# A transformer block pair on one core: first projections of two mixes on the input without the norm's factor

## The chip, the cores and the metric

One core of a Trainium2 chip runs the whole program. The metric is the device time of one execution in microseconds, here called us; lower is better. Beside the time of a whole execution there is one profiled execution, from which all rows come; their times are us from the start of its span.

## What is computed

Two transformer blocks, one behind the other, on 512 positions of 1024 features, in fp32. What matters here are the two places where a norm is followed by a projection. Cut to that:

```python
def rmsnorm(x, w):                       # rms_norm of the second block is the same
    return x * lax.rsqrt(jnp.mean(x * x, axis=-1, keepdims=True) + EPS) * w

def first_block(x, ...):
    u = rmsnorm(h, norm_mix_pre[i])
    (qa, ka, va, za, ...) = jnp.split(u @ w_in[i], offs, axis=-1)
    ya = gdn_mixer(qa, ka, va, ...)      # qkv: causal_dwconv of width 4, then silu
    ...
def second_block(x, ...):
    x = x + 0.5 * swiglu(rms_norm(x, ffn1_norm[l]), ...)
    z = rms_norm(x, mix_norm[l]) @ w_in[l] + b_in[l]
    a_q, a_k, a_v, ... = jnp.split(z, SPLIT_POINTS, axis=-1)
    ...
```

The factor `rsqrt(mean(x*x))` is one number per position; the gain `w` is one per feature. The projection sums over features, so the factor can stand ahead of the projection or behind it.

## The kernel before

**Layout.** Features lie on the 128 partitions, positions along a row: `h`, `u_hi` and `u_lo` are 8 chunks of 128 x 512. Every fp32 product is three products in a rounded format: a value is split in a high half (rounded) and a low half (the rest), and `hi*hi + hi*lo + lo*hi` is summed in a PSUM bank. `u_hi` and `u_lo` are the halves of the normed input, `w_hi` and `w_lo` those of the weights.

**Weights.** They come as a stream of slabs of 512 KB, eight 128 x 128 tiles each. SyncE (SP) loads slab s into one of four `raw` buffers (L591), when the slab four before it has been split; ScalarE rounds it to `w_hi` (L1254, `feed_to`), GpSimd (POOL) subtracts for `w_lo` (L625), TensorE may use it then. There are five split buffers. ScalarE rounds slabs at places in its queue that the code names; `feed(name, m)` rounds up to some slabs ahead of a group.

**Groups.** A group is one output chunk: 8 input chunks x 3 products of 128 x 512, 5.4 us. `dense` runs the groups of a layer one after another (L701 to L703). For layers in `ABREAST` (qkv, w_o, up, up1, wq, up2) the first four groups run abreast in four banks: for each input chunk i the products of all four (L686 to L688), so that a chunk of the input is needed only every 2.7 us. `dense(..., row=name)` puts the norm's sums ahead of step 6 and the spreading of its factor ahead of step 7 of this phase. Banks: group g uses bank g % 4 by default; TensorE waits for the reader of the bank's last group (`freed`). Banks 4 to 7 are `misc` 0 to 3. down1 ends in bank 2, `out` in bank 1.

**A norm.** ScalarE squares the chunks (L1317), VectorE adds them up (`add_squares`, L1792, which runs behind by two chunks with three buffers), TensorE sums over partitions (`row_sums`, L734), ScalarE takes the root (L1321), VectorE the reciprocal (L1769, L1820), TensorE spreads it over partitions into a bank (`row_spread`, L741). `stay_busy` (L748) is filler for TensorE.

**Two ways to use it.** At pre0 (first projection qkv) and pre3 (wq) the kernel waits for the factor: VectorE makes the product of h, gain and factor (`norm_apply`, L1779), ScalarE rounds it to `u_hi` (L1285, `split_hi`), VectorE subtracts for `u_lo` (L1783), chunk by chunk. At pre1, pre2 and pre4 (up, up1, up2) it doesn't wait: ScalarE writes `u_hi` as h times gain (L1296, `late_act`), VectorE `u_lo` (L1796, `late_lo`), the abreast phase runs, and the factor, copied to `r_sb` (L1822, `late_inverse`), multiplies the outputs (L1829). The outputs of these layers are all multiplied; nothing else reads u there.

**Behind qkv.** For each of 12 groups ScalarE copies the bank times a tap (L1355), VectorE adds three shifted taps (L1867), ScalarE does silu (L1359). For the first 8, q and k, ScalarE squares (L1367), TensorE sums over partitions (`length_sum`, L1181, called behind group m for chunk m - 2, behind group 4 for chunks 0 to 2), ScalarE copies that to `lens` (L1371). TensorE goes on with the next group only behind its sums. Then come rows1 and the delta rule (`gdn`), which reads u too (nq, nk and more projections).

**Behind wq.** VectorE adds the bias (L2173); wk goes to ScalarE (L1610), then `wv` (L720, VectorE L2177) and the attention with a window of 128.

## Time and profile before

| | us |
|---|---|
| median of 3 runs | 2319.16 (2318.23 to 2320.23) |
| profiled execution, whole time | 2319.29 |
| its span, first to last instruction | 2317.5 |
| TensorE (PE) busy | 2238.6 (97%) |
| VectorE (DVE) / ScalarE (ACT) / GpSimd (POOL) busy | 887.0 / 892.8 / 905.1 |
| mean granted TensorE clock | 0.991 of 2.4 GHz |

A timeline row is: start, duration, engine, line of the kernel, operation, output<-inputs, shapes, count; in brackets the idle time of the engine ahead of it and what ended it. PEld is TensorE's weight load, ACTq and SPq are the queues' issues of DMAs. A granted clock of 1.00 is 2.4 GHz, 0.50 is 1.2 GHz. Matmuls overlap: one of 128 x 512 is shown with 0.39 us and starts 0.227 us behind the one before it.

### The profile page before, as it was taken

The page shows a single profiled execution, that of the slowest core. Times are in us where ns is not written, and L with a number is a line of the kernel's source. Part 1 is how long each engine was busy: PE and PEld are TensorE (multiplying, and loading weights), DVE is VectorE, ACT ScalarE, POOL GpSimd, SP SyncE. Part 2 cuts the span into 40 slices and gives each one's busy share as a digit, 9 for nine tenths or more (in the row PEclk, how much of TensorE's full clock was granted, in tenths as well). Part 3 has the DMA queues.
Part 4 walks back from the last instruction along what each step waited for, and adds up shares of the span by engine and source line. Part 5 has one row for each costly group of instructions (what it writes and reads, how often), then busy time and mean ns, then how long its engine had stood idle before and what let it go on. Part 6 is the DMA issues. An engine that isn't in the chain of part 4 may idle for free.

```text
span 2317.5 us, 27646 instructions
## 1 busy us (share of the span) xinstructions
PE 2238.6 (97%) x11180; PEld 1834.1 (79%) x11180; DVE 887.0 (38%) x1561; ACT 892.8 (39%) x1479; POOL 905.1 (39%) x387
## 2 busy tenths in 40 slices
PE   7999789999999999999999999999999999999998
PEld 6789677778788888777888888767888888888887
DVE  5374444544655540225333103262645223323201
ACT  4544544554444442243322222364336433232221
POOL 3321232224454454445444443214442444444442
PEclk9999989999999999999999999999999999999999
DMA  4200231114132333222233332113331232323331
GB/s 156 82 28 28 94 118 47 55 50 134 63 108 92 99 112 92 69 91 82 91 95 105 100 99 88 55 37 101 92 100 37 82 93 90 109 91 98 99 103 46
DMA packets 54990, 197.94 MB, mean 85 GB/s; under 512 B 6352, under 2 KB 7248, under 8 KB 54480
## 3 DMA queue, kind: packets, MB, share of 16 engines
q1 hardware_dynamic: 52416, 188.77, 26.1%
q10 hardware_dynamic: 2448, 7.41, 0.9%
q8 instruction: 89, 1.46, 0.3%
q14 instruction: 37, 0.30, 0.0%
HBM read 194.06 MB, written 2.10 MB: 85 GB/s over the span
## 4 chain that ended last, share of the span: by engine, by line
PE 90%; DVE 5%; ACT 2%; issue 1%; POOL 1%; DMA 1%; ACTq 0%; SPq 0%; DVEq 0%
PE dense L701 16%; PE dense L703 16%; PE dense L702 16%; PE misc L701 5%; PE misc L702 5%; PE misc L703 5%; PE misc L662 3%; PE misc L664 2%; PE misc L663 2%; PE dense L686 1%; PE dense L687 1%; PE dense L688 1%; DVE slot L1792 1%; PE dense L827 1%; PE dense L976 1%
## 5 line engine op out<-in xcount | busy, mean ns | idle before, releaser
L625 POOL TENSOR_TENSOR w_lo<-raw,w_hi 128x1024 fp32r<-128x1024 f32 x349 | 853.8, 2459 | 1260.3 <-ACT w_hi L1254 1204.8
L1254 ACT ACTIVATE w_hi<-raw 128x1024 fp32r<-128x1024 f32 x352 | 361.8, 1050 | 159.9 <-PE dense L703 100.1
L701 PE MATMUL dense<-u_hi,w_hi 128*128 128x512 f32 x928 | 366.8, 395 | 8.6 <-DVE ug_lo L2158 7.5
L703 PE MATMUL dense<-u_hi,w_lo 128*128 128x512 f32 x928 | 361.8, 390 | 0.0
L702 PE MATMUL dense<-u_lo,w_hi 128*128 128x512 f32 x864 | 336.3, 389 | 0.0
L701 PEld LDWEIGHTS dense<-u_hi,w_hi 128*128 128x128 f32 x928 | 174.6, 188 | 50.6 <-DVE ug_lo L2158 7.9
L701 PE MATMUL dense<-a_hi,w_hi 128*128 128x512 f32 x528 | 205.4, 389 | 0.0
L702 PE MATMUL dense<-a_lo,w_hi 128*128 128x512 f32 x528 | 205.4, 389 | 0.0
L703 PE MATMUL dense<-a_hi,w_lo 128*128 128x512 f32 x528 | 205.4, 389 | 0.0
L703 PEld LDWEIGHTS dense<-u_hi,w_lo 128*128 128x128 f32 x928 | 174.6, 188 | 36.7
L702 PEld LDWEIGHTS dense<-u_lo,w_hi 128*128 128x128 f32 x864 | 162.2, 188 | 35.5 <-issue 2.4
L701 PE MATMUL misc<-u_hi,w_hi 128*128 128x512 f32 x400 | 155.8, 390 | 0.0
L702 PE MATMUL misc<-u_lo,w_hi 128*128 128x512 f32 x400 | 155.6, 389 | 0.0
L703 PE MATMUL misc<-u_hi,w_lo 128*128 128x512 f32 x400 | 155.6, 389 | 0.0
L702 PEld LDWEIGHTS dense<-a_lo,w_hi 128*128 128x128 f32 x528 | 99.1, 188 | 20.7
L703 PEld LDWEIGHTS dense<-a_hi,w_lo 128*128 128x128 f32 x528 | 99.1, 188 | 20.7
L701 PEld LDWEIGHTS dense<-a_hi,w_hi 128*128 128x128 f32 x528 | 99.1, 188 | 20.2
L1792 DVE TENSOR_TENSOR slot<-slot,slot 128x512 f32<-128x512 f32 x63 | 54.2, 860 | 142.2 <-ACT slot L1317 139.0
L1844 DVE SCALAR_TENSOR_TENSOR h<-dense,h 128x512 f32<-128x512 f32 x24 | 16.6, 692 | 240.1 <-PE dense L703 240.1
L1332 ACT ACTIVATE slot<-dense 128x512 f32<-128x512 f32 x30 | 18.0, 599 | 211.9 <-DVE dense L1829 211.9
L703 PEld LDWEIGHTS misc<-u_hi,w_lo 128*128 128x128 f32 x400 | 75.1, 188 | 15.7
L701 PEld LDWEIGHTS misc<-u_hi,w_hi 128*128 128x128 f32 x400 | 75.1, 188 | 15.6
(419 smaller groups left out, 3924.8 us busy)
## 6 DMA issues: line engine op xcount, KB each, us to landing
raw<-in_weights SPq DMA_DIRECT2D x352, 512.0 KB, 3.5
h<-in_x SPq DMA_DIRECT2D x4, 512.0 KB, 6.3
alibi<-in_alibi ACTq DMA_DIRECT2D x1, 2048.0 KB, 7.4
h<-in_x ACTq DMA_DIRECT2D x2, 1024.0 KB, 6.3
out<-result SPq DMA_DIRECT2D x8, 256.0 KB, 2.2
masks_in<-in_masks ACTq DMA_DIRECT2D x1, 512.0 KB, 9.2
p_raw<-in_p ACTq DMA_DIRECT2D x1, 512.0 KB, 3.5
mvb<-in_mvb ACTq DMA_DIRECT2D x1, 512.0 KB, 3.1
```

The lines of the kernel that those rows point to most:

```text
L625: nc.gpsimd.tensor_tensor(w_lo[:, s % SPLITS, :, :], raw[:, s % RAWS, :, :], w_hi[:, s % SPLITS, :, :].bitcast(F32), ALU.subtract).then_in ...
L662: mm(out, hi, src_hi[:, i, :], start=(i == 0), stop=False)
L663: mm(out, hi, src_lo[:, i, :], start=False, stop=False)
L664: last = mm(out, lo, src_hi[:, i, :], start=False, stop=(i == k - 1))
L686: mm(out, hi, src_hi[:, i, :], start=(i == 0), stop=False)
L687: mm(out, hi, src_lo[:, i, :], start=False, stop=False)
L688: last = mm(out, lo, src_hi[:, i, :], start=False, stop=(i == k - 1))
L701: mm(out, hi, src_hi[:, i, :], start=(i == 0), stop=False)
L702: mm(out, hi, src_lo[:, i, :], start=False, stop=False)
L703: last = mm(out, lo, src_hi[:, i, :], start=False, stop=(i == k - 1))
L1254: f(w_hi[:, s % SPLITS, :, :], raw[:, s % RAWS, :, :], ACT.Copy).then_inc(w_part, 1)
L1792: TT(slot[2][:, :], (slot[2] if c > 1 else sq[0])[:, :], sq[c % 3][:, :], ALU.add).then_inc(ms_acc, 1)
```

## The change

At qkv and at wq the abreast phase now runs on h times gain, without the factor, as at up, up1 and up2. The factor multiplies the four outputs in their banks: `first_scaled` at qkv, ahead of ScalarE's tap copy, with the new semaphore `qs_done`; at wq ahead of the bias. Unlike there, other groups and layers read u behind this phase. So `u_hi` and `u_lo` are written a second time, now with the factor (`rewrite` on VectorE, `rewrite_hi` on ScalarE), each chunk as soon as TensorE has read it in the abreast phase (`u_read`), and group 4 waits chunk by chunk for the second writing (`again`). The sums stand ahead of step 4 and the spread ahead of step 5 at qkv, 2 and 3 at wq. pre0's factor is copied to a place of its own, `r_first`.

With it: slab 0 is loaded ahead of x and slab 1 in the middle of it; masks and rowmask are issued behind the root of pre0; ScalarE waits for vec, ident and ones before its first work; the filler ahead of qkv is 6 products in place of 30, that ahead of wq is gone; qkv uses five banks, wq six, wk and wv banks of their own. All numbers of `u_ready` behind are shifted. The diff, without the shifted numbers:

```diff
+        for c in range(12):
+            bank_of[START["qkv"][1] + c] = (0, 1, 2, 3, 7)[c % 5]
+        for c in range(8):
+            bank_of[START["wq"][1] + c] = c % 6
+        for c in range(2):
+            bank_of[START["wk"][1] + c] = 2 + c
+        for c in range(NT):
+            bank_of[START["wv"][1] + c] = (4, 5, 0, 1)[c]
...
         def _(sp):
-            for i in range(4):
-                sp.dma_start(h[:, 2 * i:2 * i + 2, :], t["x"][:, 2 * i:2 * i + 2, :]).then_inc(x_loaded[i], 16)
-            for s in range(NSLABS):
-                if s >= RAWS:
-                    sp.wait_ge(*split_of(s - RAWS))
+            for s, pairs in ((0, (0, 1)), (1, (2, 3)), (2, ()), (3, ())):
+                sp.dma_start(raw[:, s, :, :], t["weights"][s]).then_inc(w_loaded[s], 16)
+                for i in pairs:
+                    sp.dma_start(h[:, 2 * i:2 * i + 2, :], t["x"][:, 2 * i:2 * i + 2, :]).then_inc(x_loaded[i], 16)
+            for s in range(RAWS, NSLABS):
+                sp.wait_ge(*split_of(s - RAWS))
...
-                            mm(out, hi, src_hi[:, i, :], start=(i == 0), stop=False)
+                            first = mm(out, hi, src_hi[:, i, :], start=(i == 0), stop=False)
+                            if again is not None and m == 0 and i >= 1:
+                                first.then_inc(u_read, 1)
...
+                        if again is not None and m == ahead:
+                            pe.wait_ge(u_ready, again + i + 1)
...
-            norm_row("pre0", busy=(16, 2, 12))
+            stay_busy(6)
...
-            dense("qkv", u_hi, u_lo, (u_ready, 0), length_sum)
+            dense("qkv", u_hi, u_lo, (u_ready, 0), length_sum, row="pre0", row_at=(4, 5), again=DC)
...
-            norm_row("pre3", busy=(8, 2, 8))
-            dense("wq", u_hi, u_lo, (u_ready, 4 * DC))
+            dense("wq", u_hi, u_lo, (u_ready, 5 * DC), row="pre3", row_at=(2, 3), again=6 * DC)
...
+            def early_act():
+                f(spare_col, one_col, ACT.Sqrt)
+                feed_to(1)
+                for c in range(DC):
+                    act.wait_ge(x_loaded[c // 2], 16)
+                    f(u_hi[:, c, :], h[:, c, :], ACT.Copy, scale=V("mix_pre", c)).then_inc(u_part, 1)
+                    square("pre0", c, h)
+                    if c in (1, 5, 7):
+                        feed_to(rounded[0] + 1)
+                root("pre0", misc[3])
+
+            def rewrite_hi(k0, name):
+                slabs = (START[name][0] + 4 * DC - 1) // SLAB + 1
+                for c in range(DC):
+                    feed_to(slabs + 1 + c // 2)
+                    act.wait_ge(ux_done, k0 + c + 1)
+                    if c < DC - 1:
+                        act.wait_ge(u_read, (DC - 1) * k0 // DC + c + 1)
+                    else:
+                        act.wait_ge(dense_done, group_of(name, 3))
                     f(u_hi[:, c, :], slot[4 + c % 2][:, :], ACT.Copy).then_inc(u_part, 1)
...
+            act.wait_ge(pool_step, 3)
+            act.wait_ge(in_loaded, 48)
+            early_act()
             act.dma_start(masks_in[:, :, :], t["masks"]).then_inc(c_loaded, 16)
             act.dma_start(rowmask[:, :], t["rowmask"]).then_inc(c_loaded, 16)
-            act.wait_ge(pool_step, 3)
-            norm_act(0, 0)
-            split_hi(0, "qkv")
+            rewrite_hi(0, "qkv")
...
+                    if c < 4:
+                        act.wait_ge(qs_done, c + 1)
                     f(slot[c % 2][:, :], out_bank("qkv", c)[:, :], ACT.Copy,
...
-            norm_act(3, 24, "down1")
-            split_hi(8, "wq")
+            late_act(3, 24, "mix2", "wq", "down1")
+            rewrite_hi(8, "wq")
...
-            def norm_apply(n, gain, k0):
-                inverse(f"pre{n}")
+            def rewrite(gain, k0, factor):
                 for c in range(DC + 1):
                     if c < DC:
                         if c >= 2:
-                            dve.wait_ge(u_ready, k0[1] + c - 1)
-                        STT(slot[4 + c % 2][:, :], h[:, c, :], V(gain, c), misc[2][:, :], ALU.mult, ALU.mult)\
+                            dve.wait_ge(u_ready, k0 + c - 1)
+                        STT(slot[4 + c % 2][:, :], h[:, c, :], V(gain, c), factor[:, :], ALU.mult, ALU.mult)\
                             .then_inc(ux_done, 1)
...
-            for i in range(4):
-                dve.wait_ge(x_loaded[i], 16)
-            for c in range(1, DC):
-                add_squares("pre0", c)
-            norm_apply(0, "mix_pre", (0, 0))
+            for c in range(DC):
+                late_lo(c, "mix_pre", 0)
+                if c >= 2:
+                    add_squares("pre0", c - 1)
+            add_squares("pre0", DC - 1)
+            late_inverse("pre0", r_first)
+            rewrite("mix_pre", DC, r_first)
+
+            def first_scaled(c):
+                dve.wait_ge(dense_done, group_of("qkv", c))
+                out = out_bank("qkv", c)
+                TT(out[:, :], out[:, :], r_first[:, :], ALU.mult).then_inc(qs_done, 1)
 
+            first_scaled(0)
             for c in range(12):
+                if c + 1 < 4:
+                    first_scaled(c + 1)
                 dve.wait_ge(cv_lin, c + 1)
...
-            add_half("down1", 0.5, "pre3")
-            norm_apply(3, "mix2", (0, 32))
+            add_half("down1", 0.5, "pre3", ("mix2", 5 * DC))
+            late_inverse("pre3")
+            rewrite("mix2", 6 * DC, r_sb)
             for c in range(8):
                 dve.wait_ge(dense_done, group_of("wq", c))
+                if c < 4:
+                    out = out_bank("wq", c)
+                    dve_link(dve, TT(out[:, :], out[:, :], r_sb[:, :], ALU.mult))
```

## Rows read from the trace of the kernel before

**Rows 1.** The page: share of each engine in the chain that ended last.
```profile
PE 90%; DVE 5%; ACT 2%; issue 1%; POOL 1%; DMA 1%; ACTq 0%; SPq 0%; DVEq 0%
```
**Rows 2.** The start: timeline, then one stretch of busy time by engine.
```profile
8.85 5.21 PE L748 MATMUL misc<-ident,ones 128*128 128x128 f32 x32 [8.85 <-DMA ones<-in_ones]
...
10.00:12.00 2.00, 2.00 (x12) 2.00 (x11) 0.74 (x2) 0.05 (x1) 0.00 (x0) 1.00 1.02 400
```
**Rows 3.** The chain behind the abreast phase of qkv; the table load; the sums.
```profile
44.48 0.70 ACT slot L1355
...
45.86 1.28 ACT L1359 ACT_TABLE_LOAD   x1
...
53.14 1.88 PE L1181 MATMUL misc<-slot,ones 128*128 128x512 f32 x4
54.26 0.63 ACT L1367 ACTIVATE slot<-qkv 128x512 f32<-128x512 f32 x1 [1.63 <-PE misc L1181]
...
56.05 0.79 PE L701 MATMUL dense<-u_hi,w_hi 128*128 128x512 f32 x1
```
**Rows 4.** VectorE by line: duration in ns, min/median/max.
```profile
L1796 DVE SCALAR_TENSOR_TENSOR u_lo<-h,vec,u_hi x24: 735/750/2866, 597.1 to 1944.6; 128x512 fp32r<-128x512 f32 x24
...
L1779 DVE SCALAR_TENSOR_TENSOR slot<-h,vec,misc x16: 740/748/751, 20.2 to 1425.0; 128x512 f32<-128x512 f32 x16
...
L1829 DVE TENSOR_TENSOR dense<-dense,r_sb x30: 693/700/700, 1071.3 to 2179.4; 128x512 f32<-128x512 f32 x30
...
L1867 DVE SCALAR_TENSOR_TENSOR slot<-dense,vec,slot x36: 737/749/752, 45.2 to 101.6; 128x511 f32<-128x511 f32 x12, 128x510 f32<-128x510 f32 x12, 128x509 f32<-128x509 f32 x12
```
**Rows 5.** Timelines: GpSimd and VectorE side by side, the steps of ScalarE, pre3's first product.
```profile
19.05 7.49 POOL L625 TENSOR_TENSOR w_lo<-raw,w_hi 128x1024 fp32r<-128x1024 f32 x3 [0.23 <-ACT w_hi L1254]
21.62 2.66 DVE L1783 TENSOR_TENSOR u_lo<-slot,u_hi 128x512 fp32r<-128x512 f32 x1
...
1057.75 2.87 DVE L1796 SCALAR_TENSOR_TENSOR u_lo<-h,vec,u_hi 128x512 fp32r<-128x512 f32 x1
...
1943.89 0.72 ACT L1296 ACTIVATE u_hi<-h,vec 128x512 fp32r<-128x512 f32 x1 [3.25 <-DVE h L1844]
...
1945.04 1.04 ACT L1254 ACTIVATE w_hi<-raw 128x1024 fp32r<-128x1024 f32 x1
...
1415.55 1.41 DVE L1779 SCALAR_TENSOR_TENSOR slot<-h,vec,misc 128x512 f32<-128x512 f32 x2 [1.25 <-PE misc L741]
...
1425.64 1.48 DVE L1783 TENSOR_TENSOR u_lo<-slot,u_hi 128x512 fp32r<-128x512 f32 x2
```
**Rows 6.** Stretches: length; PE, PEld, DVE, ACT, POOL busy (x); granted clock; DMA share; GB/s.
```profile
24.34:46.31 21.97, 21.97 (x96) 17.86 (x96) 11.27 (x15) 8.46 (x12) 9.29 (x4) 1.00 0.40 121
289.24:295.06 5.82, 5.82 (x27) 5.82 (x28) 5.73 (x8) 1.77 (x2) 2.39 (x1) 0.50 0.62 187
1063.06:1069.89 6.83, 6.83 (x21) 5.67 (x21) 0.18 (x1) 4.38 (x5) 4.62 (x2) 0.50 0.17 53
1410.39:1418.08 7.69, 6.50 (x54) 5.93 (x52) 4.62 (x8) 3.10 (x5) 2.36 (x1) 1.00 0.01 3
1418.08:1439.97 21.89, 21.89 (x97) 18.13 (x98) 10.61 (x16) 7.93 (x10) 9.51 (x4) 1.00 0.39 113
1472.60:1473.75 1.15, 0.17 (x2) 0.03 (x1) 0.00 (x0) 0.94 (x2) 0.00 (x0) 1.00 0.81 224
1942.96:1967.01 24.05, 23.94 (x114) 19.73 (x113) 5.30 (x9) 7.18 (x9) 8.09 (x5) 1.00 0.21 64
619.33:622.74 3.41, 3.41 (x11) 2.83 (x11) 0.18 (x1) 2.80 (x4) 1.52 (x1) 0.50 0.00 0
```
**Rows 7.** Waits between wk and wv: engine line waited for: us, times, longest.
```profile
PE dense L720 <- ACT wk L1610: 1.0, 1, 1.0
```
**Rows 8.** Timeline: sums, and the copy of the factor, at pre1.
```profile
618.64 1.26 PE L734 MATMUL misc<-ones,slot 128*128 128x1 f32 x8 [3.34 <-DVE slot L1792]
...
625.08 0.69 DVE L1822 COPY r_sb<-misc 128x512 f32<-128x512 f32 x1 [4.67 <-PE misc L741]
```

More of the change, by code:

```diff
@@ L242, in build @@
         r_sb = arena("r_sb", 86, [S])
+        r_first = arena("r_first", 24, [S])
         p_raw = at("p_raw", 88 * KB, [2, S])
@@ L314, in build @@
         u_ready = sem("u_ready")
+        u_read = sem("u_read")
+        qs_done = sem("qs_done")
         po_copy = sem("po_copy")
@@ L667, in dense_part, with dense @@
                     last.then_inc(dense_done, 1)
-            def dense(name, src_hi, src_lo, k_ready=None, after=None, row=None):
+            def dense(name, src_hi, src_lo, k_ready=None, after=None, row=None, row_at=(DC - 2, DC - 1), again=None):
                 tile, g0 = START[name]
@@ L675, in dense @@
                     for i in range(k):
-                        if row and i == k - 2:
+                        if row and i == row_at[0]:
                             row_sums(row, misc[3])
-                        if row and i == k - 1:
+                        if row and i == row_at[1]:
                             row_spread(row, misc[3])
@@ L1199, in _ @@
             norm_row("post0", busy=(6, 2, 14))
-            dense("up", u_hi, u_lo, (u_ready, DC), row="pre1")
+            dense("up", u_hi, u_lo, (u_ready, 2 * DC), row="pre1")
             dense("down", a_hi, a_lo, (a_ready, 0))
@@ L1208, in _ @@
             for m in range(DC):
-                dense(f"ple_gate{m}", u_hi, ug_lo, (u_ready, 2 * DC) if m == 0 else None)
+                dense(f"ple_gate{m}", u_hi, ug_lo, (u_ready, 3 * DC) if m == 0 else None)
                 if 1 <= m < DC - PLE_AHEAD + 1:
@@ L1213, in _ @@
             norm_row("post2", busy=(10, 2, 14))
-            dense("up1", u_hi, u_lo, (u_ready, 3 * DC), row="pre2")
+            dense("up1", u_hi, u_lo, (u_ready, 4 * DC), row="pre2")
             dense("down1", a_hi, a_lo, (a_ready, FC))
-            norm_row("pre3", busy=(8, 2, 8))
-            dense("wq", u_hi, u_lo, (u_ready, 4 * DC))
+            dense("wq", u_hi, u_lo, (u_ready, 5 * DC), row="pre3", row_at=(2, 3), again=6 * DC)
             dense("wk", u_hi, u_lo)
@@ L1236, in _ @@
             dense("out", mg_hi, mg_lo, (mg_ready, 0))
-            dense("up2", u_hi, u_lo, (u_ready, 5 * DC), row="pre4")
+            dense("up2", u_hi, u_lo, (u_ready, 7 * DC), row="pre4")
             dense("down2", a_hi, a_lo, (a_ready, 2 * FC))
@@ L1270, in norm_act @@
                         feed(layer, c)
-                    if n == 0:
-                        act.wait_ge(x_loaded[c // 2], 16)
-                    else:
-                        act.wait_ge(h_ready, ready + c + 1)
-                    square(f"pre{n}", c, h)
-                if n == 0:
-                    feed_to(1)
-                root(f"pre{n}")
-            def split_hi(k0, name):
-                feed_to((START[name][0] + 4 * DC - 1) // SLAB + 1)
-                for c in range(DC):
-                    act.wait_ge(ux_done, k0 + c + 1)
+                    act.wait_ge(h_ready, ready + c + 1)
+                    square(f"pre{n}", c, h)
+                root(f"pre{n}")
+            def early_act():
[15 more added lines that the diff above has]
+                        act.wait_ge(u_read, (DC - 1) * k0 // DC + c + 1)
+                    else:
+                        act.wait_ge(dense_done, group_of(name, 3))
                     f(u_hi[:, c, :], slot[4 + c % 2][:, :], ACT.Copy).then_inc(u_part, 1)
@@ L1363, in _ @@
                     if i == 0:
-                        act.wait_ge(u_ready, 8)
+                        act.wait_ge(u_ready, 2 * DC)
                     if i >= 2:
@@ L1814, in post_apply, with late_inverse @@
                         add_squares(pre, c - 2)
-            def late_inverse(name):
+            def late_inverse(name, factor=r_sb):
                 r = NORMS.index(name)
@@ L1821, in late_inverse @@
                 dve.wait_ge(ms_row, r + 1)
-                dve_link(dve, v.tensor_copy(r_sb[:, :], misc[3][:, :]))
+                dve_link(dve, v.tensor_copy(factor[:, :], misc[3][:, :]))
             def ffn_gate(n, name):
@@ L1871, in _ @@
             dve.wait_ge(c_loaded, 32)
-            dve.wait_ge(u_ready, 8)
+            dve.wait_ge(u_ready, 2 * DC)
             dve_link(dve, v.tensor_copy(masks[:, :, :], masks_in[:, :, :]))
@@ L2165, in _ @@
             add_squares("post2", DC - 1)
-            post_apply(2, "ple_post", mo_a, "pre2", "ffn1", 3 * DC)
+            post_apply(2, "ple_post", mo_a, "pre2", "ffn1", 4 * DC)
             late_inverse("pre2")
             ffn_gate(1, "up1")
-            add_half("down1", 0.5, "pre3")
-            norm_apply(3, "mix2", (0, 32))
+            add_half("down1", 0.5, "pre3", ("mix2", 5 * DC))
+            late_inverse("pre3")
+            rewrite("mix2", 6 * DC, r_sb)
             for c in range(8):
                 dve.wait_ge(dense_done, group_of("wq", c))
+                if c < 4:
+                    out = out_bank("wq", c)
+                    dve_link(dve, TT(out[:, :], out[:, :], r_sb[:, :], ALU.mult))
                 TS(wq[:, c, :], out_bank("wq", c)[:, :], V("b_wq", c), ND ** -0.5, ALU.add, ALU.mult).then_inc(wq_done, 1)
@@ L2356, in _ @@
                 TT(mg_lo[:, m, :], ma[:, m, :], mg_hi[:, m, :].bitcast(F32), ALU.subtract).then_inc(mg_ready, 1)
-            add_half("out", 0.5, "pre4", ("ffn2", 5 * DC))
+            add_half("out", 0.5, "pre4", ("ffn2", 7 * DC))
             late_inverse("pre4")
```

7 lines of the change are left out of this document (3 added, 4 removed).

## The prediction

> **What bounds the kernel.** The page first: TensorE is 90% of the chain that ended last [rows 1]. So a change pays only where TensorE stands still, or where something in front of a standing TensorE becomes shorter or longer. I then read the chain and the timeline at the two places that the change touches.
>
> At the start, TensorE waits for the `ones` load until 8.85 us [rows 2], does filler and the sums of pre0, and begins its first projection at 24.34. It does the four abreast groups in 21.97 us [rows 6], then group 4 (the fifth), and then, from 53.14, the three length sums. These wait for what VectorE and ScalarE make of groups 0 to 2: the chain of work that ended last runs through the tap copy L1355 at 44.48 [rows 3]. Group 5 begins at 56.05. From there to rows1 TensorE hardly stands, so the start of group 5 is my milestone for stage one. Its inputs: group 0 ready at 44.48, group 5 at 56.05, 11.57 us later.
>
> Before wq TensorE has its last `down1` product issued at 1410.39 and its first wq product at 1418.08: 7.69 us, filler included, then 21.89 us for the abreast phase, and 1.15 us between wk and wv [rows 6], most of it a wait for `wk` [rows 7]. The clock was granted in full in all of these stretches.
>
> **Stage two: what goes.** It becomes what the kernel already does from `out` to up2: there the abreast phase with sums and spread inside it took 24.05 us from the last product of `out` [rows 6], with no idle time ahead. Of that some 0.3 us was a wait for bank 1, which `out` had just used and up2 wants with its fourth product (an estimate: a sum of 0.7 on VectorE less the 0.45 of TensorE's products in between); down1 ends in bank 2, wanted with the seventh, so I take 23.7. Against 7.69 + 21.89 = 29.58 that is 5.9 us less. The rewrite begins behind the spread at product step 3 and must be ahead of group 4. By the steps below it takes 18 us from `r_sb` and that is ready about 11 us into the phase: the last halves come at 29.0, while group 4 wants them at 23.7 + 7 x 0.68 = 28.5. I take 0.5 us off the gain: 5.4. The four extra products on VectorE (0.70 us each, L1829 [rows 4]) and the wq bias behind them are done at about 35.5; group 6, the first that wants their bank, comes at 35.1 but needs only the first of the four. The new banks free wv of the wait for `wk`: 1.0 us. **Stage two: -6.4 us** (bounds -7.9, if the sums inside the phase cost nothing more than their 1.05 us and nothing waits, and -4.5, if the rewrite is 2 us later).
>
> **Stage one, the start.** SyncE now sends slab 0 first. The loads move about 400 GB/s [rows 2], 1.3 us for 512 KB, so the last pair of x, 2.1 MB into SyncE's queue before, comes at most two slabs, 2.6 us, later; it is there by 14 (an estimate), and ScalarE wants it only at about 18: nothing. ScalarE's work waits for `ones`, 8.85; a table load was done in the idle time ahead of another wait (45.86 [rows 3]), so I count it as done; if not, 1.28 us more. Then 0.2 + 1.0 (`w_hi`), pairs of `u_hi` and square of 1.15 us (1943.89 to 1945.04), and `w_hi` of 1.04 after the second, sixth and eighth pair [rows 5].
>
> GpSimd splits slab 0 from 10.15 to 12.5. And here is what I hold for decisive: **VectorE instructions with both inputs in SBUF and GpSimd's split keep each other out.** `u_lo` L1783, 0.74 us for one of two at the end of pre3, took 2.66 at 21.62, beside the splits from 19.05 to 26.54; L1796, 0.75 in the median, took 2.87 at 1057.75. As three splits in a row took 7.49, with one VectorE instruction let in between two of them, I take it that they take turns, a split being 2.4. Instructions with an input in PSUM, L1779, L1829, L1867, never took longer than 0.752 [rows 4, 5]. Laid out in this way: first `u_lo` at 13.1 (held by split 0), second 13.8, third 16.7 (held by split 1), first add 17.3, for which square 3 waits 2.3 us. ScalarE's last square ends at 8.85 + 0.2 + 3 x 1.0 + 8 x 1.15 + 2.3 = 23.6. VectorE's sixth add ends about 25.0, split 3 holds the port to 27.3, then `u_lo`, add, add: **29.1**. TensorE starts at 13.2, 11.1 us earlier, is through four of the eight steps at 13.2 + 4 x 2.73 = 24.1, and stands before the sums until 29.1. Bounds: 24.1 (no turn lost) and 30.4.
>
> **Sums to factor.** From sums to the end of the copy of the factor took 7.13 us at 618.64 (to 625.77), behind an idle time of 3.34 us [rows 8] and with the clock at half, 1.2 GHz, for 3.41 us of work [rows 6]. At full clock that would be 1.7 less, 5.4; with the half clock of 6.83 us that pre2 shows [rows 6] 8.8. Here TensorE has stood 5.0. I take 7.1: **36.2**.
>
> **The rewrite.** Eight times product (0.75), `u_hi` copy and `u_lo` (0.74): 11.6 us in all from 1415.55 to 1427.12 [rows 5], 1.4 a chunk. But the product read the factor from PSUM; now it reads `r_first`, so all of VectorE's rewrite has both inputs in SBUF. ScalarE rounds a slab ahead of chunks 2, 4 and 6, so GpSimd splits three slabs (2.4 us each) in the middle of it, each keeping VectorE out for nearly all of its time: 7.2, less the 1.0 in which VectorE would have waited for ScalarE anyway: 6.2, total 18.0. (The slab ahead of chunk 0, and the 1.4 us of issuing masks and rowmask, now in ScalarE's queue behind the root, lie before the factor.) Bounds 11.6 and 19. **54.2**.
>
> **From rewrite to group 5.** VectorE takes its queue in order: the first scaling, and with it every convolution, stands behind the last `u_lo`. Then the old chain of 11.57 us with 0.70 for the first scaling, 1.4 for two more between the convolutions, less the 1.63 us in which square 2 had waited for TensorE [rows 3], which it now doesn't, and 0.3 for the silus behind: 12.3. Meanwhile TensorE ends its abreast groups near 44 and group 4 with the last halves at about 55, then stands for 11 us but for single sums. **Group 5: 66.5**, 10.5 later than 56.05. At 289.24 TensorE came back from a long idle time to a half clock for 5.82 us of work [rows 6], which costs half of that, 2.9 (bounds 0 and 3.4). **Stage one: +13.4.** rows1 now waits for group 10's convolution, a copy of 0.70 and three of 0.75 behind its group [rows 3, 4], within the 5.4 us that group 11 takes: nothing.
>
> **Sum.** The profiled execution took 2319.29 us, 0.13 over the median of 2319.16, with a span of 2317.5. 2319.3 + 13.4 - 6.4 = **2326.3**.
>
> **Rules of the Trainium skill.** L1796 takes 0.750 us with `h` and `u_hi` in SBUF, L1779 0.748 with one source in PSUM [rows 4]. The Trainium skill, Vector Engine (DVE) Microarchitecture Reference, section Points that are easy to get wrong, says that this form with two SBUF sources that aren't bf16 runs at half the rate. By that the product of the rewrite would slow down; the trace speaks against it.
>
> **Rivals.**
> - The forecast, locks and turns as laid out, 2324 to 2332: 0.55.
> - Part of the turns fall between VectorE's instructions: sums at 27, factor 5.45 behind, rewrite 15, group 5 at 59.8, clock 1.7: +5.4 - 6.4, 2318.3, and what lies within 4.6 us of before. For it: half of the instructions at L1796 took 0.75 or less [rows 4], in stretches in which GpSimd worked too. 0.25.
> - The other side: the new order of GpSimd and VectorE meets hardly at all. Sums 24.1, factor 29.6, rewrite over at 41.2, group 5 at 53.5, clock 1.7: -0.8 - 6.4, **2312.1**. It decides through the end of the rewrite: with 12.3 and 2.9 behind it and 6.4 gained in stage two, the change wins if that end is before 56.05 + 6.4 - 15.2 = 47.3. 0.12.
> - The rewrite's cover holds also for the scalings (VectorE gets them done without holding up TensorE), so that the abreast phase alone decides: 13.2 + 23.7 = 36.9 against 46.31, -9.4 - 6.4: 2303.5. The order of VectorE's queue speaks against it. 0.04.
> - The product with both sources in SBUF takes double, 8 x 0.75 = 6.0 more in the rewrite: 2332.3. Against it stands L1796 [rows 4]. 0.04. (It is what the rule of the Trainium skill above would do.)
>
> **Range and chances.** 4.6 us is 0.2% and about what a measurement can tell. Faster by more: 0.12 + 0.04 less rounding, 0.15; within: 0.25; slower by more: 0.55 + 0.04, 0.60. The range goes from the fast rival, 2311, to 2332 and leaves out 2303.5, the doubled product and the tail of my bounds.
>
> **What would show it.** In the new profile: first L686 near 13.2; sums of pre0 near 29 with 5 us of idle TensorE ahead and a half clock around it; the copy of `r_first` near 36; some of the rewrite's products or `u_lo` at 2 to 3 us instead of 0.75; first scaling near 54; TensorE idle between group 4 and group 5, whose first product is near 66. Near wq: no idle behind down1, wv right behind wk. I am wrong if all instructions of the rewrite take 0.75 us, or if group 5 starts before 60.

## The result and the profile after

The changed kernel takes **2322.93 us** (median of 20 runs, 2319.66 to 2325.80), the kernel before 2318.93 (20 runs beside them, 2316.82 to 2320.37). Ratio 1.0017, 95% interval 1.0011 to 1.0023: 4.0 us or 0.17% slower. The profiled execution of after has a span of 2321.4 us where before had 2317.5, at a mean granted clock of 0.987.

Only two places of the program changed their length by more than the clock makes. I follow one and the same weight slab through both traces, by the start of its rounding on ScalarE (`w_hi`, L1254 before, L1268 after), and subtract:

```
slab   before     after      after - before
18     130.15     142.17     +12.0   behind stage one (qkv, rows1)
42     375.75     388.90     +13.2
210   1396.90    1408.54     +11.6   ahead of stage two
228   1527.92    1531.88      +4.0   behind stage two (wq, wk, wv)
359   2277.34    2281.31      +4.0   last slab
```

Stage one costs 12.0 us, stage two gives 7.7 by this measure, and what lies between wanders by 1.5.

**The start.** Timelines of after: ScalarE, VectorE, GpSimd and TensorE; start, duration, engine, line, operation, in brackets the idle time ahead and what ended it.

```profile
8.81 1.28 ACT L1291 ACT_TABLE_LOAD   x1 [8.81 <-DMA ones<-in_ones]
...
18.32 0.63 ACT L1343 ACTIVATE slot<-h 128x512 f32<-128x512 f32 x1 [2.11 <-DVE slot L1820]
...
11.90 3.00 DVE L1824 SCALAR_TENSOR_TENSOR u_lo<-h,vec,u_hi 128x512 fp32r<-128x512 f32 x2 [2.90 <-ACT u_hi L1295]
15.11 2.58 DVE L1824 SCALAR_TENSOR_TENSOR u_lo<-h,vec,u_hi 128x512 fp32r<-128x512 f32 x1 [0.21 <-ACT u_hi L1295]
...
18.21 0.74 DVE L1824 SCALAR_TENSOR_TENSOR u_lo<-h,vec,u_hi 128x512 fp32r<-128x512 f32 x1
...
22.82 2.38 DVE L1824 SCALAR_TENSOR_TENSOR u_lo<-h,vec,u_hi 128x512 fp32r<-128x512 f32 x1 [0.60 <-ACT u_hi L1295]
...
25.73 2.87 DVE L1824 SCALAR_TENSOR_TENSOR u_lo<-h,vec,u_hi 128x512 fp32r<-128x512 f32 x1
...
11.33 2.35 POOL L636 TENSOR_TENSOR w_lo<-raw,w_hi 128x1024 fp32r<-128x1024 f32 x1 [10.89 <-ACT w_hi L1268]
14.54 2.60 POOL L636 TENSOR_TENSOR w_lo<-raw,w_hi 128x1024 fp32r<-128x1024 f32 x1 [0.85 <-ACT w_hi L1268]
...
22.25 2.40 POOL L636 TENSOR_TENSOR w_lo<-raw,w_hi 128x1024 fp32r<-128x1024 f32 x1 [5.12 <-ACT w_hi L1268]
25.48 2.57 POOL L636 TENSOR_TENSOR w_lo<-raw,w_hi 128x1024 fp32r<-128x1024 f32 x1 [0.82 <-ACT w_hi L1268]
...
14.30 0.79 PE L697 MATMUL dense<-u_hi,w_hi 128*128 128x512 f32 x1 [2.58 <-DVE u_lo L1824]
14.89 0.63 PE L700 MATMUL dense<-u_lo,w_hi 128*128 128x512 f32 x1
...
30.05 1.05 PE L749 MATMUL misc<-ones,slot 128*128 128x1 f32 x8 [2.73 <-DVE slot L1820]
```

Four of the eight `u_lo` take long: 2.34 at 11.90 (the first of the two in that row), 2.58 at 15.11, 2.38 at 22.82 and 2.87 at 25.73. Each starts within 0.6 us behind the start of a split; where GpSimd is idle, at 18.21, one takes 0.74. TensorE starts 10 us earlier than at 24.34 [rows 6] and then stands 2.73 us ahead of the sums. The sums themselves come at 30.05.

**The rewrite and what follows.** The same engines, where before the chain of [rows 3] ran:

```profile
36.48 0.69 DVE L1850 COPY r_first<-misc 128x512 f32<-128x512 f32 x1 [4.86 <-PE misc L756]
37.21 1.41 DVE L1807 SCALAR_TENSOR_TENSOR slot<-h,vec,r_first 128x512 f32<-128x512 f32 x2
...
40.77 2.77 DVE L1807 SCALAR_TENSOR_TENSOR slot<-h,vec,r_first 128x512 f32<-128x512 f32 x1
43.46 0.68 DVE L1811 TENSOR_TENSOR u_lo<-slot,u_hi 128x512 fp32r<-128x512 f32 x1
...
50.35 2.73 DVE L1807 SCALAR_TENSOR_TENSOR slot<-h,vec,r_first 128x512 f32<-128x512 f32 x1
53.01 1.46 DVE L1811 TENSOR_TENSOR u_lo<-slot,u_hi 128x512 fp32r<-128x512 f32 x2
54.39 1.29 DVE L1896 TENSOR_TENSOR dense<-dense,r_first 128x512 f32<-128x512 f32 x2
...
40.31 2.68 POOL L636 TENSOR_TENSOR w_lo<-raw,w_hi 128x1024 fp32r<-128x1024 f32 x1 [4.80 <-ACT w_hi L1268]
45.23 2.54 POOL L636 TENSOR_TENSOR w_lo<-raw,w_hi 128x1024 fp32r<-128x1024 f32 x1 [2.24 <-ACT w_hi L1268]
50.01 2.52 POOL L636 TENSOR_TENSOR w_lo<-raw,w_hi 128x1024 fp32r<-128x1024 f32 x1 [2.24 <-ACT w_hi L1268]
...
59.59 2.07 PE L1196 MATMUL misc<-slot,ones 128*128 128x512 f32 x2 [4.10 <-ACT slot L1396]
62.41 2.07 PE L1196 MATMUL misc<-slot,ones 128*128 128x512 f32 x2 [0.75 <-ACT slot L1396]
65.80 2.05 PE L1196 MATMUL misc<-slot,ones 128*128 128x512 f32 x2 [1.32 <-ACT lens L1400]
66.86 1.42 PE L716 MATMUL dense<-u_hi,w_hi 128*128 128x512 f32 x1
```

The rewrite goes from 37.21 to 54.47, 17.3 us. Three of its eight products take 2.7 to 2.8 us, each beside one of the three splits; the other products take 0.75 and all `u_lo` 0.68 or 0.69. Behind it stand the first scaling at 54.39 and then, one after another, the three length sums L1196, each for a square L1396 or a `lens` copy. Group 5 starts at 66.86, where before it started at 56.05 [rows 3].

**Stage two.** TensorE, VectorE and GpSimd of after, then the abreast phase as a stretch (length; busy time of PE, PEld, DVE, ACT, POOL; clock, DMA share, GB/s):

```profile
1426.86 0.95 PE L749 MATMUL misc<-ones,slot 128*128 128x1 f32 x8
1430.54 1.05 PE L756 MATMUL misc<-ident,small 128*128 128x128 f32 x8
1445.06 0.39 PE L716 MATMUL misc<-u_hi,w_hi 128*128 128x512 f32 x1
...
1431.62 0.69 DVE L1850 COPY r_sb<-misc 128x512 f32<-128x512 f32 x1 [3.30 <-PE misc L756]
1435.92 2.77 DVE L1807 SCALAR_TENSOR_TENSOR slot<-h,vec,r_sb 128x512 f32<-128x512 f32 x1
1448.20 1.47 DVE L1811 TENSOR_TENSOR u_lo<-slot,u_hi 128x512 fp32r<-128x512 f32 x2
...
1435.46 2.68 POOL L636 TENSOR_TENSOR w_lo<-raw,w_hi 128x1024 fp32r<-128x1024 f32 x1 [3.95 <-ACT w_hi L1268]
...
1421.42:1445.06 23.64, 23.64 (x113) 19.81 (x112) 16.10 (x19) 9.85 (x15) 10.48 (x4) 1.00 0.28 77
```

No PE row carries a bracket: TensorE runs from down1 into wq and on into group 4 without standing. It takes 23.64 us where before took 7.69 + 21.89 [rows 6], 5.94 less. The rewrite has the same three slow products and is over 17.3 us behind its start (1432.35 to 1449.67), and here nobody waits for it: group 4 wants the last chunk at 1445.06 + 7 x 0.68 = 1449.8, 0.15 us later.

### The profile page after: what moved, and what is told of

Its sections match the earlier page's. It is cut to its first block, busy times and chain, and to the rows that moved or that the text cites. A ratio compares the mean times of both kernels' runs of the same rounds, so it can differ in the third digit from the quotient of the medians.

```text
span 2321.4 us, 27525 instructions
## 1 busy us (share of the span) xinstructions
PE 2236.2 (96%) x11096; PEld 1826.8 (79%) x11096; DVE 919.2 (40%) x1587; ACT 901.2 (39%) x1495; POOL 905.2 (39%) x387
## 4 chain that ended last, share of the span: by engine, by line
PE 89%; DVE 6%; ACT 2%; issue 1%; POOL 1%; DMA 0%; ACTq 0%; DVEq 0%
PE dense L716 15%; PE dense L718 15%; PE dense L717 15%; PE misc L716 5%; PE misc L718 5%; PE misc L717 5%; PE misc L673 3%; PE misc L675 2%; PE misc L674 2%; PE dense L697 1%; PE dense L701 1%; PE dense L700 1%; DVE slot L1820 1%; PE dense L842 1%; PE dense L991 1%
## 5 line engine op out<-in xcount | busy, mean ns | idle before, releaser
L1268 ACT ACTIVATE w_hi<-raw 128x1024 fp32r<-128x1024 f32 x352 | 362.2, 1050 | 143.4 <-PE dense L718 87.2
L716 PE MATMUL dense<-u_hi,w_hi 128*128 128x512 f32 x896 | 354.7, 396 | 7.5 <-DVE ug_lo L2196 7.5
L718 PE MATMUL dense<-u_hi,w_lo 128*128 128x512 f32 x896 | 349.6, 390 | 0.0
L717 PE MATMUL dense<-u_lo,w_hi 128*128 128x512 f32 x832 | 324.1, 390 | 0.0
L716 PEld LDWEIGHTS dense<-u_hi,w_hi 128*128 128x128 f32 x896 | 168.7, 188 | 47.9 <-DVE ug_lo L2196 7.9
L718 PEld LDWEIGHTS dense<-u_hi,w_lo 128*128 128x128 f32 x896 | 168.8, 188 | 35.4
L716 PE MATMUL misc<-u_hi,w_hi 128*128 128x512 f32 x432 | 169.1, 391 | 4.5 <-DVE u_lo L1811 4.5
L717 PE MATMUL misc<-u_lo,w_hi 128*128 128x512 f32 x432 | 168.2, 389 | 0.0
L718 PE MATMUL misc<-u_hi,w_lo 128*128 128x512 f32 x432 | 168.1, 389 | 0.0
L716 PEld LDWEIGHTS misc<-u_hi,w_hi 128*128 128x128 f32 x432 | 81.1, 188 | 23.0 <-DVE u_lo L1811 6.2
L718 PEld LDWEIGHTS misc<-u_hi,w_lo 128*128 128x128 f32 x432 | 81.1, 188 | 17.0
```

Of the source, the lines that this page charges most:

```text
L716: mm(out, hi, src_hi[:, i, :], start=(i == 0), stop=False)
L717: mm(out, hi, src_lo[:, i, :], start=False, stop=False)
L718: last = mm(out, lo, src_hi[:, i, :], start=False, stop=(i == k - 1))
L1268: f(w_hi[:, s % SPLITS, :, :], raw[:, s % RAWS, :, :], ACT.Copy).then_inc(w_part, 1)
```

## The experiments

Each kernel ran 5 to 11 times, beside the kernel before, but for the last one, `wv_banks`, of which there is one execution. Behind each time I give the drift: how much later slabs 18 and 228 come than in before, read as in the table above. It belongs to the profiled execution and not to the median; the profiled one of `second_only` was the fastest of its seven (2310.09). Beside the first four the median of before was 2319.53, beside the next four 2319.96, beside `factor_psum` 2319.36.

### One place alone

`second_only` keeps the first mix as before, `first_only` the second:

```diff
 first_only, against the changed kernel
-            dense("wq", u_hi, u_lo, (u_ready, 5 * DC), row="pre3", row_at=(2, 3), again=6 * DC)
+            norm_row("pre3", busy=(8, 2, 8))
+            dense("wq", u_hi, u_lo, (u_ready, 5 * DC))
...
-            late_act(3, 24, "mix2", "wq", "down1")
-            rewrite_hi(8, "wq")
+            norm_act(3, 24, "down1")
+            split_hi(8, "wq")
```

> Only the second mix (wq) is changed; the first stays as before. In the traces of before and after the same places of the program lie 12.0 us later behind qkv, 11.0 before wq and 4.0 behind wv: so the second part is worth -7.0. My theory: it is independent of the first, 2318.9 - 7.0 = 2311.9, and wq's product steps run without idle time behind down1. Rival: some of the 7 us is given by the shifted position in time (the clock periods fell differently between the two traces, by 1.2 us and back): then 2313 to 2315.

> Only the first mix (qkv) is changed; wq stays as before. My theory: +12.0, 2330.9, the whole loss. Rival, that the two parts act together (the shifted start changes what wq meets): the sum of this run's and of second_only's difference to before would not be the +4.0 of the whole change; mine says that it is within 1 us.

Measured: `second_only` 2313.42 (ratio 0.9971, 0.9960 to 0.9981), drift -0.1 and -9.3; `first_only` 2331.53 (1.0049, 1.0037 to 1.0062), drift +12.3 and +12.1. In `second_only` 1.4 us of the drift arose between the two stages, where the code is that of before (slab 210: -1.5), so stage two is worth 7.7 there, as by the same measure in the changed kernel. (The median is 1.5 us over what I had expected of it, that of `first_only` 0.6.) I had asked that the parts add up to the whole, +4.0, within 1 us. By the medians they give -6.1 + 12.0 = +5.9, by the drifts -9.3 + 12.1 = +2.8: off by 1.9 and 1.2, on either side. The interval of `second_only` alone is 2.4 us to each side, so an effect of one part on the other of 1 or 2 us is neither shown nor excluded. What is shown is that the small whole is the difference of a loss of about 12 and a gain of 6 to 8, and that stage two alone beats both kernels.

### The splits inside the rewrite

`slabs_later`: in the first mix ScalarE rounds no slab ahead of chunks 2, 4 and 6 of the rewrite, so GpSimd splits none in it.

```diff
-                    feed_to(slabs + 1 + c // 2)
+                    feed_to(slabs + 1 + (c // 2 if k0 else 0))
```

> The changed kernel, but in the first mix ScalarE rounds slabs 5, 6 and 7 only behind the rewrite, so GpSimd splits none of them beside it. Lock theory: the three products of the rewrite that took 2.73 to 2.77 us take 0.75, the rewrite 11.6 instead of 17.3; the two slabs then stand ahead of ScalarE's first tap copy and cost back about 0.7 to 1.4: 2322.9 - 4.6 = 2318.3. Rival, that these products are slow for their two SBUF sources: they stay at 2.75 and the time rises by about 1, to 2324.

```profile
33.26 2.37 POOL L636 TENSOR_TENSOR w_lo<-raw,w_hi 128x1024 fp32r<-128x1024 f32 x1 [5.10 <-ACT w_hi L1268]
47.28 4.67 POOL L636 TENSOR_TENSOR w_lo<-raw,w_hi 128x1024 fp32r<-128x1024 f32 x2 [11.65 <-ACT w_hi L1268]
...
35.72 1.42 DVE L1807 SCALAR_TENSOR_TENSOR slot<-h,vec,r_first 128x512 f32<-128x512 f32 x2
...
44.84 0.75 DVE L1807 SCALAR_TENSOR_TENSOR slot<-h,vec,r_first 128x512 f32<-128x512 f32 x1
45.51 1.47 DVE L1811 TENSOR_TENSOR u_lo<-slot,u_hi 128x512 fp32r<-128x512 f32 x2
```

These are GpSimd's and VectorE's timelines of `slabs_later`: 11.65 us without a split, and in them the whole rewrite, 35.72 to 46.98 = 11.3 us, no product over 0.75. 2319.59 (0.9998, 0.9989 to 1.0007), drift +5.7 and -1.2: 3.3 us faster than the changed kernel by the medians (4.6 expected), 6.3 us less drift behind stage one. Not all of the 6.3 is the splits: the copy of the factor came 1.5 us earlier (34.99 for 36.48), since no half clock lay between the sums and it, and a half clock from 53.87 to 64.11 then lay on 4.4 us of group 5, which started at 59.72. That the splits take 6 us of the rewrite is shown by the length of the rewrite itself. It also settles the price of a product with both sources in SBUF: 0.75, as with one in PSUM (L1779, 0.748 [rows 4]).

`no_rewrite` leaves out the second writing in the first mix (groups from 4 on, rows1 and the delta rule then read the input without the factor):

> The changed kernel without the second writing of u in the first mix: its 24 instructions are left out (two small ones keep the order), so everything behind the first four groups of qkv reads u without the factor and the result is not the reference's. Theory, that the rewrite standing in VectorE's queue ahead of the scalings is the loss: group 5 starts 12.3 us behind the end of the first abreast groups, near 55.5 instead of 66.9, and the time is 2322.9 - 11.4 = 2311.5. Rival, that the late sums and factor or the extra scalings are the loss: group 5 stays behind 60 and the time above 2316.

```profile
42.37 1.38 DVE L1907 TENSOR_TENSOR dense<-dense,r_first 128x512 f32<-128x512 f32 x2 [4.73 <-PE dense L701]
...
53.79 1.10 PE L1196 MATMUL misc<-slot,ones 128*128 128x512 f32 x2 [2.27 <-ACT lens L1405]
```

VectorE and TensorE of `no_rewrite`: the first scaling now waits for TensorE and comes at 42.37 in place of 54.39, the third length sum at 53.79 in place of 65.80, each 12.0 earlier. Group 5 starts at 54.33. 2311.48 (0.9965, 0.9952 to 0.9979), drift +0.7 and -7.8. So what follows moves by the same 12.0 from the scaling to the last length sum, and of stage one's 12.0 only 0.7 is left without the rewrite: stage one's loss is the rewrite.

`factor_psum` asks which instructions the split holds up:

```diff
-            bank_of[START["qkv"][1] + c] = (0, 1, 2, 3, 7)[c % 5]
+            bank_of[START["qkv"][1] + c] = (0, 1, 2, 3, 6)[c % 5]
...
-            rewrite("mix_pre", DC, r_first)
+            rewrite("mix_pre", DC, misc[3])
```

> The changed kernel, but in the first mix the rewrite's product (VectorE) reads the factor where TensorE spread it, in PSUM bank 7, and not its copy r_first in SBUF; for that the fifth bank of qkv is 6 in place of 7. So the product has one input in SBUF, and only u_lo has two. In the changed kernel three of the eight products took 2.75 us instead of 0.75, each beside one of GpSimd's splits, and the rewrite 17.3 us. Theory (an instruction with two inputs in SBUF waits for the split; one with an input in PSUM does not): no product over 0.8 us; the splits then hold the u_lo that follows instead, up to three of them near 2 us; the rewrite takes 15 to 17 us, group 5 starts at 64.5 to 66.6. Rival 1 (only the product's third operand was the trouble, u_lo with its two SBUF inputs passes, as all eight did in the changed kernel at 0.68): rewrite 11.6, group 5 near 61, some 5.5 us less: 2317.5. Rival 2 (any VectorE instruction is held, whatever it reads): products at 2.75 as in the changed kernel.

VectorE and GpSimd of `factor_psum`:

```profile
40.74 0.75 DVE L1807 SCALAR_TENSOR_TENSOR slot<-h,vec,misc 128x512 f32<-128x512 f32 x1
41.41 2.12 DVE L1811 TENSOR_TENSOR u_lo<-slot,u_hi 128x512 fp32r<-128x512 f32 x1
43.56 0.75 DVE L1807 SCALAR_TENSOR_TENSOR slot<-h,vec,misc 128x512 f32<-128x512 f32 x1
44.22 2.12 DVE L1811 TENSOR_TENSOR u_lo<-slot,u_hi 128x512 fp32r<-128x512 f32 x1
...
40.28 2.69 POOL L636 TENSOR_TENSOR w_lo<-raw,w_hi 128x1024 fp32r<-128x1024 f32 x1 [4.67 <-ACT w_hi L1268]
43.19 2.61 POOL L636 TENSOR_TENSOR w_lo<-raw,w_hi 128x1024 fp32r<-128x1024 f32 x1 [0.21 <-ACT w_hi L1268]
```

The product at 40.74 starts 0.46 us into a split, as the one at 40.77 in the changed kernel does, and takes 0.75 in place of 2.77: its one difference is a source in PSUM. The `u_lo` behind it, which never was slow in the changed kernel, now is, beside each of the three splits (2.12, 2.12 and 2.07). The rewrite takes 15.3 us (37.18 to 52.48), group 5 starts at 64.88. This is as the theory had it, and both rivals fall. The Trainium skill, SBUF — State Buffer, section SBUF: two separate sides, has VectorE and GpSimd share ports that one of them holds exclusively; the rows agree, and it is the inputs in SBUF that count. The whole time, 2323.41 (1.0018, 1.0009 to 1.0028), doesn't show these 2 us; the drift behind stage one (+10.4 for +12.0) does.

### The order of the length sums

Three idle times ahead of length sums stand before group 5. `sums_later` puts them behind later groups:

```diff
-                for c in range(0 if m == 4 else m - 2, min(m - 1, 8)):
+                upto = {3: 0, 4: 0, 5: 2, 6: 4}
+                for c in range(min(upto.get(m - 1, m - 3), 8), min(upto.get(m, m - 2), 8)):
```

> The changed kernel with one edit: the length sums of q and k (TensorE) come one group or more later: those of chunks 0 and 1 behind group 5, 2 and 3 behind group 6, then one behind each group; none ahead of group 5. It tests what held group 5 at 66.9 us. Theory (the wait is the order of TensorE's own queue: group 5 stands behind three length sums, the last of which needs the second, third silu and square behind the rewrite, while group 5's bank wants only the convolution of group 0): group 5 starts about 3.8 us behind the last halves of the rewrite (one scaling 0.7, tap copy 0.75, three convolution steps 2.3), near 58.3 instead of 66.9, group 6 near 64.6 instead of 74.4; what follows is 9 to 10 us earlier, 2313. Rival (VectorE's queue behind the rewrite is the bound whoever asks first: groups 5 to 7 each wait for a convolution, so that only some 3 us come back by group 8): 2319 to 2320.

> The changed kernel with two edits at once: length sums later as in sums_later, and in the first mix no slab split ahead of chunks 2, 4 and 6 of the rewrite as in slabs_later (one ahead of it only). Theory (the two costs add: the splits hold up the rewrite by 6.2 us, the order of the sums costs another 9): rewrite over at 47.0, group 5 near 51.1, group 6 near 57.4, 17 us earlier than in the changed kernel: 2306, faster than both kernels. Rival (without the sums in front, TensorE itself is the bound: group 4 and the half clock end what can be had, and slabs that come late are missed): group 6 not before 62, 2310 or more.

TensorE of `sums_later`, the last wait for halves and then group 5:

```profile
54.84 0.49 PE L716 MATMUL misc<-u_hi,w_hi 128*128 128x512 f32 x1 [2.41 <-DVE u_lo L1812]
59.37 0.80 PE L716 MATMUL dense<-u_hi,w_hi 128*128 128x512 f32 x1 [2.66 <-DVE slot L1906]
```

and of `both_later`:

```profile
54.33 0.70 PE L716 MATMUL dense<-u_hi,w_hi 128*128 128x512 f32 x1 [2.56 <-DVE slot L1906]
61.52 1.88 PE L1197 MATMUL misc<-slot,ones 128*128 128x512 f32 x4
```

Group 5 of `sums_later` starts at 59.37, 3.8 us behind the end of the rewrite (55.56), and waits only for the convolution that frees bank 0: the theory's wait and the theory's 3.8. But the kernel takes 2317.81 (0.9992, 0.9983 to 1.0001), 5.1 us less than the changed kernel where 9 to 10 were expected, drift +7.4 and +0.1. That lies between the theory and the rival, which had 2319 to 2320 and some 3 us left by group 8. Against the changed kernel group 5 is 7.5 us earlier (its factor copy began 1.1 us later, at 37.57, with a half clock ahead of it), group 6 6.4 (68.01 for 74.42) and groups 7 and 8 5.6 (75.21 for 80.77). Two sums stand behind group 5 and two behind group 6, one more each than in the changed kernel, and one costs 0.9 us (groups with one sum behind them follow each other in 6.35, their 24 products take 5.4); these two I had left out. By slab 18 it is 4.6. The last 0.9 us goes in all three kernels with this order: it is the eighth sum, which now stands behind group 10 and not behind group 9. In `old_fixed`, below, the lead over before is 3.7 us at groups 8 and 10 and 2.8 at rows1 (96.28 for 99.11).

`both_later` takes 2310.80 (0.9961, 0.9949 to 0.9974), drift +2.2 and -7.1. It beats both kernels, but the numbers are those of the rival (group 6 not before 62, 2310 or more) and not of the theory (51.1, 57.4, 2306): group 5 starts at 54.33, group 6 at 62.83. Its rewrite is 11.3 us, as in `slabs_later`, but began 3.2 us later (38.91 for 35.72), again behind a half clock between the sums and the factor; a half clock and the two sums then follow group 5's start. The rival's reason holds in part only: in front of group 5 TensorE stood 2.56 us for the convolution, so there it was VectorE and not TensorE that set the time.

### The first mix as before, mended

The trace of before has a gap of its own. VectorE adds the squares of pre0 only when all of x is there; and group 5 stands behind the length sums. `old_adds` is `second_only` with the first mended, `old_fixed` adds the five banks and the new order of the sums.

```diff
 old_adds, against second_only
+            for c in range(1, DC):
+                add_squares("pre0", c)
             for i in range(4):
                 dve.wait_ge(x_loaded[i], 16)
-            for c in range(1, DC):
-                add_squares("pre0", c)
```

> second_only (the first mix as before, the second as changed) with one edit: VectorE no longer waits for all of x before it adds the first squares. Before, it waited for the whole of x; the sums of pre0 came at 16.7 us, though the squares of the first chunks were there long before. Theory (the additions then follow ScalarE's squares chunk by chunk): sums near 14.1, first product of qkv near 21.8 instead of 24.3, and all behind it 2.5 us earlier than in second_only: 2311. Rival (the last pair of x and its square set the sums, not the additions): sums within 1 us of before, 2312.5 to 2313.5.

> old_adds with two more edits of the first mix that need nothing of its change: five banks for qkv as in the changed kernel, and the length sums later as in sums_later. Theory (before, TensorE stood in front of group 5 for the length sums, the start of group 5 was 56.05 while group 4 was through at 53.1): group 5 near 49.3 and group 6 near 55.7, where before it was 62.4; time 2305 to 2307. Rival (group 5 then waits for the convolution of group 0, and the ones behind it for VectorE, so that most of the 6.7 us returns as waits by group 8): 2309 or more.

TensorE of `old_adds`:

```profile
14.68 0.95 PE L745 MATMUL misc<-ones,slot 128*128 128x1 f32 x8
...
22.25 0.50 PE L693 MATMUL dense<-u_hi,w_hi 128*128 128x512 f32 x1 [2.11 <-DVE u_lo L1805]
```

`old_adds`: 2311.94 (0.9966, 0.9954 to 0.9979). The sums are 2.0 us earlier than at 16.68, the first product 2.1, but the half clock that in before fell on filler now falls on projections (products 0.43 us apart from 23.88), group 5 is 0.5 us earlier than in before (55.52), and in this execution the drift is -0.6 at slab 18. The medians give 1.5 us against `second_only`, from another set of runs; the gain is not settled. `old_fixed`: **2308.94** (0.9954, 0.9942 to 0.9967), the fastest of all, 11.0 us under before, drift -2.8 and -10.1. Its group 5 follows group 4 without a gap at 51.05, 5.0 us earlier than in before (expected 49.3), group 6 is at 57.80 (expected 55.7), and group 8 is 3.7 us earlier than in before (71.36 for 75.08). So the rival was nearer here: part of the gain returns, but the whole is still 11 us, of which stage two brings 7.7.

### The banks of wk and wv

`wv_banks` is the kernel before with the banks of wq, wk and wv alone.

> The kernel before with the banks of wq, wk and wv of the changed kernel, and nothing else. It tests the term of 1.0 us that I gave to these banks. Theory: the 1.15 us between wk and wv (TensorE's wait for a bank that ScalarE has yet to read) are gone, wv starts some 1.0 us earlier counted from the first product of wq. Rival (ScalarE's reading of wk is needed for something else ahead of wv or right behind, so the gap only moves): the same time from wq's first product to the first scores of the window.

```profile
1473.98 0.39 PE L709 MATMUL dense<-u_hi,w_lo 128*128 128x512 f32 x1
1474.21 0.28 PE L726 MATMUL misc<-w_hi,u_hi 128*128 128x256 f32 x1
```

wv's first product starts 0.23 us behind wk's last, without the wait of [rows 7]. Drift +1.6 at slab 210 and +0.4 at 228: 1.2 us, as the theory had it, and it is still there behind the window. The one time, 2319.71 us, can't show it.

## Why the prediction was right, and where it wasn't

The sign and the place of each cost were right. The sum of 2326.3 was 3.0 us over the profiled execution (2323.29) and 3.4 over the median (2322.93). The most likely case was not hit: slower by more than 4.6 us had 0.60, and the +4.0 fell among the results that I had tied to partial turns, at 0.25, a mechanism that did not come. The 3.0 us are 1.7 of clock behind the rewrite and 1.0 between the stages that I did not have and 0.6 more gain in stage two, less 0.3 more loss up to group 5. Two small slips in the working carried little: 11.6 and 6.2 for the rewrite make 17.8 and not 18.0, and the outer bound of stage two comes out as -7.6 from 7.69 less 1.05 and the 1.0 of the banks, not -7.9.

**The start.** First product 14.30 for 13.2: the table load stood at 8.81 behind the waits, the case that I had named with 1.28 us and counted as nothing. The term that failed is the reading of [rows 3], that a table load is done in the idle time ahead of its activation's wait. There one wait stood ahead of the activation, here two; whether that makes the difference no run tests. The turns of GpSimd and VectorE came as laid out: square 3 waited 2.11 for 2.3, sums 30.05 for 29.1, the difference being the table load less 0.3. TensorE stood 2.73 ahead of them instead of 5.0, since it began 1.1 later and its first products came 0.43 us apart for about 3.5 us (14.89 on) instead of 0.23. That cost nothing: the sums set the end.

**Sums to factor.** 30.05 to 37.17 = 7.12 for 7.1. The three cases that I had named all came in some kernel: 5.52 us in `slabs_later` without a half clock (30.16 to 35.68, for 5.4), 7.12 here with 3.4 us of it, and 8.71 in `both_later` with 6.8 us (30.16 to 38.87, for 8.8). The prices hold; that the changed kernel met the middle one was luck.

**The rewrite.** 17.3 for 18.0. The mechanism holds, and in `factor_psum` and `slabs_later` it is shown. The term of 6.2 for the splits measured 6.0 (17.3 less 11.3).

**Rewrite to group 5.** 54.47 to 66.86 = 12.4 for 12.3, though 0.5 of it is the half clock on the last length sum (65.80 to 66.86, in before 55.52 to 56.05). `sums_later` shows what is in it: 3.8 us for the bank, the rest for the order of the length sums.

**The half clock behind.** I took 2.9 us. The stretch of after (columns as above) answers:

```profile
59.23:69.47 10.24, 7.81 (x11) 3.28 (x12) 8.88 (x13) 7.62 (x13) 0.55 (x1) 0.50 0.00 1
```

The half clock lay from 59.23 to 69.47: it began in the 4.10 us in which TensorE stood for the first length sum (59.59), and ended 2.6 us into group 5: group 5 with its sum took 7.56 us (66.86 to 74.42) against 6.34 in before (56.05 to 62.39). 1.2 us, not 2.9. This is the largest mis-sized term. I had priced the clock by the working part of a stretch [rows 6]. The whole of that stretch of before shows the same 10.24 us of half clock:

```profile
284.82:295.06 10.24, 5.82 (x27) 5.85 (x28) 5.73 (x8) 6.03 (x9) 5.44 (x3) 0.50 0.77 271
```

There 5.82 us of it lay on dense work; here three quarters (59.23 to 66.86) lay on waiting and single sums, and 2.6 us on group 5. Stage one: +12.0 for +13.4.

**Stage two.** -7.0 for -6.4, from the last product of down1 to the first scores of the window (1421.42 to 1490.04 against 1410.39 to 1486.09 is -7.1). The 0.5 us for late halves didn't come: I had them at 29.0 us into the phase with 28.5 wanted; they came at 28.25 (1449.67). wv gave 1.1 for 1.0.

**Between the stages.** I had taken nothing; the drift went from +12.0 to +11.6 at slab 210 and, counted by TensorE's last down1 product, to +11.0. So 12.0 - 1.0 - 7.0 = 4.0.

**The rivals.** Partial turns (2318.3): no turn was missed in the rewrite, and at the start four `u_lo` of eight met a split. The ground for its 0.25 was a misreading of [rows 4]: of L1796's 24 instructions in before only two start with more than 0.2 us of a split to go (613.85 and 1057.75), and both took 2.87 us. Those at 0.75 met at most the last 0.1 us of one, so they said nothing for partial turns. No meeting at all (2312.1): `slabs_later` comes nearest, with the rewrite's end at 46.98, just inside my 47.3 for break-even, and it is even with before at 2319.59. The point at which the change wins was right within what the runs can tell. The scalings under the rewrite's cover (2303.5): excluded, the first came at 54.39, behind the last `u_lo`. Doubled product: excluded, 0.75. By the rule of the Trainium skill, Vector Engine (DVE) Microarchitecture Reference, section Points that are easy to get wrong, it would have been 1.5 (an estimate, twice the 0.75); the rows disagree.

## What to carry to other kernels

A factor that is taken off the critical path pays where nothing else is queued behind the repair: the same rewrite of 17.3 us cost 12 us at qkv, where every convolution stands behind it in VectorE's queue, and nothing at wq, where four scalings and the bias do. The moment differs too: at wq the rewrite began 10.9 us into the abreast phase (1432.35) and ended in time for group 4's last chunk, at qkv it began 22.9 us into it (37.21) and ended 10 us behind the start of group 4 (44.48). No run separates the two. Ask of each repair what is next on its engine, and keep GpSimd's work on SBUF away from it; or leave the one place as it was and take the other alone. When TensorE stands in front of a group, look whether it stands for the group's own bank or for small products that the program queued ahead of it.

## What the runs showed of the hardware

**The exclusion goes by where the inputs lie.** Of instructions started inside a split of 2.5 to 2.7 us, a product with two sources in SBUF took 2.77, the same product with one in PSUM 0.75. The one that is held ends about 0.55 us behind the split (43.54 for 42.99), 0.2 less than its own 0.75, so it runs about as the split ends, and each costs up to 2 us. It works the other way too: 20 times in before a split begins some 0.02 us ahead of VectorE's product L2142, both inputs in SBUF (first 639.50 and 639.52); there the product takes its 0.68 and the split 2.95 to 2.98 in place of 2.40.

**The half clock wanders.** In code that is the same in all kernels the period near 325 to 335 us is 6.8 in before and 13.7 in after, the one near 1063 to 1076 is 6.8 and 3.4; summed over the granted clock of all stretches but the last 20 us, the profiled execution of before has 38 us of half clock, that of after 55, `first_only` 68, `second_only` 34. Each us of it on which TensorE works costs half a us, so two executions of equal schedules may differ by some us, and single terms of 1 to 2 us are to be read from the trace and not from the whole time.

**The column of the granted clock says nothing at the very start.** In after it gives 1.00 from 14.30 to 18.00, where the products come 0.43 us apart, twice the 0.23 of full clock. The trace of after holds no clock record before 18.27, and where there is none the column shows 1.00. In `first_only` and `sums_later` the records begin at 11.95, and a spell of products 0.43 us apart, from 15.4 to 18.8, is shown as 0.50. There it is the spacing of the products that tells.
